# One core: the first RMS norm's factor moves from x to the outputs of two projections

## The reference

```python
def rms_norm(x, w, eps=NORM_EPS):
    xf = x.astype(jnp.float32)
    y = xf * lax.rsqrt(jnp.mean(xf * xf, axis=-1, keepdims=True) + eps)
    return (y * w.astype(jnp.float32)).astype(x.dtype)
...
        xn = rms_norm(h, norm_mix_pre[i])
        z = xn @ w_in[i]
        z_rwkv, z_gla = z[..., :RWKV_IN_WIDTH], z[..., RWKV_IN_WIDTH:]
        z_rwkv = z_rwkv + rwkv_mu[i] * (centred_shift(z_rwkv) - z_rwkv)
```

## Time and profile before

| what | value |
|---|---|
| median of 3 runs | 2900.9 us (2898.66 to 2914.93) |
| the profiled execution | 2904.88 us |
| its span | 2903.0 us |
| PE busy | 2746.3 us, 95% |
| VectorE busy | 1656.2 us, 57% |
| ScalarE busy | 1220.4 us, 42% |
| first matmul | 20.75 us |
| second block of `gla_project` begins on PE | 50.45 us |
| `rwkv_project`'s first matmul | 329.41 us |

### The profile page before, as it was taken

How to read it: one execution, slowest core, us unless ns; L and a number is a source line. 1 busy time by engine, 2 the same in 40 slices (tenths; PEclk the granted TensorE clock), 3 DMA queues, 4 the chain that set the end, 5 groups by cost and what they waited for, 6 DMA issues and landing times.

```text
span 2903.0 us, 57455 instructions
## 1 busy us (share of the span) xinstructions
PE 2746.3 (95%) x24688; PEld 2253.6 (78%) x24688; DVE 1656.2 (57%) x2482; ACT 1220.4 (42%) x2232; POOL 351.5 (12%) x472
## 2 busy tenths in 40 slices
PE   4997899898998999999999999999999999999997
PEld 3776677788886788788888888788887878888886
DVE  5669667345554566756543437675446765654343
ACT  4676666222322455433333335432235544333331
POOL 2000023444541001101000000000000100100000
PEclk9997899899998999999999999999999999999999
DMA  3420244211110334433344332222223443334432
GB/s 135 144 79 3 91 140 167 76 39 38 40 28 24 126 129 174 141 131 124 116 149 161 108 109 95 87 88 101 95 95 117 178 149 119 125 115 149 166 131 87
DMA packets 137821, 317.17 MB, mean 109 GB/s; under 512 B 13216, under 2 KB 40480, under 8 KB 137568
## 3 DMA queue, kind: packets, MB, share of 16 engines
q1 hardware_dynamic: 115344, 236.94, 24.1%
q0 software_dynamic: 22224, 76.56, 7.4%
HBM read 267.18 MB, written 46.14 MB: 108 GB/s over the span
## 4 chain that ended last, share of the span: by engine, by line
PE 62%; DVE 3%; DMA 1%; issue 1%; ACT 1%; POOL 0%; DVEq 0%; SPq 0%; ACTq 0%; POOLq 0%
PE be_ps L3297 20%; PE be_ps L3328 16%; PE be_ps L3223 16%; PE be_ps L3276 7%; PE be_ps L3350 1%; PE be_ps L2792 1%; DMA f_inner<-be_gate 0%; PE be_ps L2786 0%; ACT be_whi L3385 0%; DVE ext L2850 0%; DVE big L2829 0%; PE be_ps L2411 0%; DVE be_raw_r L3634 0%; DVE big L2819 0%; DMA be_raw<-in_w_out 0%
## 5 line engine op out<-in xcount | busy, mean ns | idle before, releaser
L3634 DVE TENSOR_TENSOR be_raw_r<-be_raw,be_whi 128x1024 fp32r<-128x1024 f32 x229 | 280.4, 1224 | 477.2 <-ACT be_whi L3385 476.9
L3385 ACT CAST be_whi<-be_raw 128x1024 fp32r<-128x1024 f32 x229 | 240.4, 1050 | 566.2 <-DMA be_raw<-in_ffn_down 298.2
L3328 PE MATMUL be_ps<-ext_r,be_whi 128*128 128x512 f32 x1152 | 356.4, 391 | 0.0
L3223 PE MATMUL be_ps<-ext_r,be_whi 128*128 128x512 f32 x896 | 278.9, 392 | 5.8 <-DVE be_raw_r L3634 3.1
L3297 PE MATMUL be_ps<-ext_r 128*128 128x512 f32 x832 | 278.3, 392 | 1.4 <-DVE be_ring L3708 1.4
L3328 PEld LDWEIGHTS be_ps<-ext_r,be_whi 128*128 128x128 f32 x1152 | 216.7, 188 | 44.8
L3297 PE MATMUL be_ps<-mid_r,ext_r 128*128 128x512 f32 x704 | 225.7, 396 | 1.3 <-DVE be_ring L3708 1.3
L3328 PE MATMUL be_ps<-ext_r,be_raw_r 128*128 128x512 f32 x576 | 224.7, 390 | 0.0
L3223 PEld LDWEIGHTS be_ps<-ext_r,be_whi 128*128 128x128 f32 x896 | 166.8, 188 | 45.4 <-DVE be_raw_r L3634 4.2
L3223 PE MATMUL be_ps<-big_r,be_whi 128*128 128x512 f32 x640 | 198.8, 392 | 0.0
L3297 PEld LDWEIGHTS be_ps<-ext_r 128*128 128x128 f32 x832 | 156.1, 188 | 38.6 <-DVE be_ring L3708 1.8
(11 more groups left out here) (412 smaller groups left out, 5531.2 us busy)
## 6 DMA issues: line engine op xcount, KB each, us to landing
be_raw<-in_ffn_down SPq DMA_DIRECT2D x88, 512.0 KB, 3.4
be_raw<-in_conv_in SPq DMA_DIRECT2D x48, 512.0 KB, 3.2
ext<-f_inner SPq DMA_DIRECT2D x72, 256.0 KB, 3.7
ext<-in_ffn_gate SPq DMA_DIRECT2D x30, 512.0 KB, 4.9
ext<-in_ffn_up SPq DMA_DIRECT2D x30, 512.0 KB, 4.1
gp_ada<-in_ada POOLq DMA_DIRECT2D x24, 512.0 KB, 3.6
rp_ada<-in_ada POOLq DMA_DIRECT2D x24, 512.0 KB, 3.9
be_raw<-in_ffn_gate SPq DMA_DIRECT2D x44, 256.0 KB, 2.7
```

What stands on the lines that cost most here:

```text
L3223: mm = pe.matmul(ps[:, bank], part[:, k * P:(k + 1) * P], xs(k), start=(k == order[0] and i == 0), stop=(k == order[-1] and i == 2))
L3328: mm = pe.matmul(ps[:, steps.bank[n, g]], part[:, at], x, start=(i % NPAIR == 0 and u == 0 and p == 0), stop=(i % NPAIR == NPAIR - 1 and u ...
L3385: act.copy(w.hi[:, n % 3], w.raw[:, n % 3]).then_inc(w.hi_ready, 1)
L3634: dve.tensor_tensor(w.lo(n), w.raw[:, n % 3], w.hi[:, n % 3].bitcast(F32), ALU.subtract).then_inc(w.lo_ready, 1)
```

## The change

x is loaded in eight pieces of two channel tiles, behind the vectors and the first weights and ahead of the constants. `xn_hi` and `xn_lo` are made from x times gain alone, so that PE's first tile does not wait for the norm. The squares, sums and roots are made beside PE's first two tiles, and the factor of each token is copied to `scale`, 128 by 1024. Each tile that leaves the banks is multiplied by `scale` on VectorE: in `gla_project` that takes the place of ScalarE's emptying (a gate's Silu then works in place), and in `rwkv_project` too, where `edge` now has one buffer, and ScalarE's multiplication by half of mu comes behind GpSimd's addition. `pre_norm` and `load_constants` as blocks are gone. The distribution of `ada` tiles over the steps of `gla_project` is another. The diff, cut to its core:

```diff
-def pre_norm(core, w, source, h, gain, xn_hi, xn_lo, c, acc):
...
+class FirstNorm:
...
+    def load(self, sp, hf, q):
+        pair = slice(2 * q, 2 * q + 2)
+        sp.dma_start(self.h[:, pair, self.cols(hf)], self.source[:, pair, self.cols(hf)]).then_inc(self.loaded[hf][q], 16)
+
+    def hi(self, act, hf, m):
+        act.wait_ge(self.loaded[hf][m // 2], 16)
+        act.activation(self.xn_hi[:, m, self.cols(hf)], self.h[:, m, self.cols(hf)], ACT.Copy, scale=self.gain[:, m:m + 1]
+                       ).then_inc(self.hi_done, 1)
+
+    def lo(self, dve, hf, m):
+
+        dve.wait_ge(self.hi_done, KD * hf + m + 1)
+        dve.scalar_tensor_tensor(self.xn_lo[:, m, self.cols(hf)], self.h[:, m, self.cols(hf)], self.gain[:, m:m + 1],
+                                 self.xn_hi[:, m, self.cols(hf)].bitcast(F32), ALU.mult, ALU.subtract
+                                 ).then_inc(self.lo_done, 1)
+
+    def square(self, act, hf, m):
+        act.activation(self.squares[hf][m], self.h[:, m, self.cols(hf)], ACT.Square).then_inc(self.squared, 1)
...
+    def take(self, act, hf):
+        act.wait_ge(self.spread, hf + 1)
+        act.copy(self.scale[:, self.cols(hf)], self.side[:, hf]).then_inc(self.scaled, 1)
...
@@ gla_project @@
-        modulation = Modulation(core, ctx, "gp", dram_ada, c, mod, 0, (3, 3, 2, 2, 2, 2, 2, 3, 0, 0, 3, 2), 9)
+        modulation = Modulation(core, ctx, "gp", dram_ada, c, mod, 0, (0, 1, 2, 2, 2, 3, 3, 3, 1, 1, 3, 3), 9)
...
+            sp.dma_start(core.vec[:, :], dram_vec).then_inc(norm.vec_loaded, 16)
+            load_weights(0)
+            for hf in two:
+                for q in range(KD // 2):
+                    norm.load(sp, hf, q)
+            load_weights(1)
+            sp.dma_start(core.const[:, :], dram_const[:, 0:N_STAY * P]).then_inc(norm.const_loaded, 16)
...
-            def drain(s):
-                act.wait_ge(filled, s + 1)
...
+            def finish_gate(s):
+                act.wait_ge(drained, s + 1)
+                act.activation(z[:, place(s)], z[:, place(s)], ACT.Silu)
...
+            weights_hi(0)
+            for hf in two:
+                for m in range(KD):
+                    norm.hi(act, hf, m)
+            weights_hi(1)
+            for m in range(KD):
+                norm.square(act, 0, m)
+            weights_hi(2)
+            for m in range(4):
+                norm.square(act, 1, m)
+            act.wait_ge(norm.const_loaded, 16)
+            norm.take_root(act, 0)
+            for m in (4, 5):
+                norm.square(act, 1, m)
+            norm.take(act, 0)
+            for m in (6, 7):
+                norm.square(act, 1, m)
+            norm.take_root(act, 1)
+            norm.take(act, 1)
+            for n in modulation.of_step(1):
+                modulation.scale(act, n)
...
+            def drain(s, hf=None):
+
+                part = slice(0, T) if hf is None else norm.cols(hf)
+                out = edge[:, s % 2, 1:T + 1] if is_conv(s) else z[:, place(s)]
+                dve.wait_ge(filled, s + 1)
+                dve.wait_ge(norm.scaled, 2 if hf is None else hf + 1)
+                ins = dve.tensor_tensor(out[:, part], acc[:, s % 2, part], scale[:, part], ALU.mult)
+                if hf != 0:
+                    ins.then_inc(drained, 1)
...
+            for s in range(2, n_tiles + 1):
                 if s + 1 < n_tiles:
                     weights_lo(s + 1)
...
+                drain(s - 1)
...
+            pool.wait_ge(norm.hi_done, 2 * KD)
             modulation.load(pool, 0, modulation.count)
...
@@ rwkv_project @@
-        edge = sb("edge", [P, 2, T + 2])
+        edge = sb("edge", [P, T + 2])
...
-            def drain(s):
-                act.wait_ge(filled, s + 1)
-                if s >= 2:
-                    act.wait_ge(summed, s - 1)
-                act.activation(edge[:, s % 2, 1:T + 1], acc[:, s % 2], ACT.Identity, scale=share[:, 1, ORDER[s]:ORDER[s] + 1]
-                               ).then_inc(edged, 1)
+            def share_around(s):
+                out = z[:, PLACE[ORDER[s]]]
+                act.wait_ge(summed, s + 1)
+                act.activation(out, out, ACT.Identity, scale=share[:, 1, ORDER[s]:ORDER[s] + 1]).then_inc(shared, 1)
...
+                if s == 7:
+                    decay_rates(2, 1)
                 if s:
-                    drain(s - 1)
+                    share_around(s - 1)
...
+            def drain(s):
+
+                dve.wait_ge(filled, s + 1)
+                if s:
+                    dve.wait_ge(summed, s)
+                    dve.wait_ge(mixed, s)
+                dve.tensor_tensor(edge[:, 1:T + 1], acc[:, s % 2], scale[:, :], ALU.mult).then_inc(edged, 1)
+
             def mix(s):
                 out = z[:, PLACE[ORDER[s]]]
-                dve.wait_ge(summed, s + 1)
-                dve.scalar_tensor_tensor(out, acc[:, s % 2], share[:, 0, ORDER[s]:ORDER[s] + 1], out, ALU.mult, ALU.add
+                dve.wait_ge(shared, s + 1)
+                dve.scalar_tensor_tensor(out, edge[:, 1:T + 1], share[:, 0, ORDER[s]:ORDER[s] + 1], out, ALU.mult, ALU.add
                                          ).then_inc(mixed, 1)
...
                 if s + 1 < NZR:
                     weights_lo(s + 1)
+                if s:
+                    drain(s - 1)
...
                 if s >= 2:
-                    pe.wait_ge(mixed, s - 1)
+                    pe.wait_ge(edged, s - 1)
```

More of the change, by code:

```diff
@@ L275, in parts @@
                                 for x in ("whi", "wlo"))
-        def flat(x):
-            return x[:, 0].rearrange("p k c -> p (k c)")
-        self.ahead = Ahead([(self.weights[self.first], flat(self.raw), flat(self.w_hi), flat(self.w_lo), self.loaded[0],
-                             self.hi_ready, self.lo_ready)])
     def w_hi_of(self, m):
@@ L731, in accumulate @@
                 dve.tensor_tensor_scan(x, mask, x, 0.0, ALU.mult, ALU.add).then_inc(summed, 1)
-            for s in range(n_tiles + 1):
+            dve.memset(edge[:, :, :], 0.0).then_inc(edged, 1)
+            dve.wait_ge(norm.vec_loaded, 16)
+            weights_lo(0)
+            for hf in two:
+                for m in range(KD):
+                    norm.lo(dve, hf, m)
+            weights_lo(1)
+            for m in range(1, KD):
+                norm.add(dve, 0, m)
+            for m in (1, 2, 3):
+                norm.add(dve, 1, m)
+            norm.invert(dve, 0)
+            for m in (4, 5):
+                norm.add(dve, 1, m)
+            drain(0, 0)
+            for m in (6, 7):
+                norm.add(dve, 1, m)
+            weights_lo(2)
+            norm.invert(dve, 1)
+            drain(0, 1)
+            for n in modulation.of_step(1):
+                modulation.add(dve, n)
+            dve.wait_ge(edged, 1)
+            for s in range(2, n_tiles + 1):
                 if s + 1 < n_tiles:
                     weights_lo(s + 1)
-                if s == 0:
-                    dve.memset(edge[:, :, :], 0.0).then_inc(edged, 1)
-                if s == 2:
-                    dve.wait_ge(edged, 1)
+                drain(s - 1)
                 if s == 10:
@@ L774, in decay_sum @@
                               ).then_inc(unit_made, 1)
-            for s in range(n_tiles):
+            pe.wait_ge(w.lo_ready, 1)
+            for hf in two:
+                for k in range(KD):
+                    pe.wait_ge(norm.lo_done, hf * KD + k + 1)
+                    for part_w, x in ((w.w_hi, xn_hi), (w.w_hi, xn_lo), (w.w_lo, xn_hi)):
+                        ins = pe.matmul(half(acc[:, 0], hf), part_w[:, 0, k], half(x[:, k], hf),
+                                        start=(k == 0 and part_w is w.w_hi and x is xn_hi),
+                                        stop=(k == KD - 1 and part_w is w.w_lo))
+            ins.then_inc(filled, 1)
+            for s in range(1, n_tiles):
                 pe.wait_ge(w.lo_ready, s + 1)
@@ L1187, in rwkv_project @@
         first_hi, fed_early, exp_table = sem("first_hi"), sem("fed_early"), sem("exp_table")
[L1188 removed]
+        filled, edged, summed, shared, mixed = (sem(x) for x in ("filled", "edged", "summed", "shared", "mixed"))
         ready, lora_loaded, keep_loaded, spread_loaded = (sem(x) for x in ("ready", "lora_loaded", "keep_loaded", "spread_loaded"))
```

234 lines of the change are left out of this document (68 added, 166 removed).

## The result

| what | before | changed |
|---|---|---|
| median of the runs made side by side (4 each) | 2905.6 us (2898.7 to 2914.9) | 2945.1 us (2943.2 to 2947.6) |
| the profiled execution, its span | 2904.9, 2903.0 us | 2944.3, 2942.5 us |
| PE busy | 2746.3 us, 95% | 2767.3 us, 94% |

The changed kernel takes 1.0131 times as long, with a 95% interval of 1.0110 to 1.0153. The forecast was 2931 us within 2908 to 2950, slower with a chance of 0.81. Sign and range held; the point lay 14 us low.

The account below looks back on a forecast made before the run. PE, busy 95% of the span, was taken as the bound. 2904.9-10.1 (front and gla_project)+37.5 (rwkv_project)+2.5 (clock) = 2934.8 us for the profiled execution, less 4.0 to the median: 2931 us, range 2908 to 2950.

Parts of the forecast that it names:

- The front: From the loads of x to tile 2 of gla_project: tile 2 begins at 39.0 us, 32.0 us earlier.
- gla_project: From tile 2 on, VectorE's longer rounds make PE wait; of the front's 32.0 us, 10.1 are left.
- the three places named: PE's waits in gla_project ahead of tiles 8, 9 and 12: 4.5, 6.7 and 4.1 us.
- rwkv_project: Longer chain through emptying, GpSimd and ScalarE's sharing: PE waits of 36.2 us and 1.3 for the tail, 37.5 lost.
- the carried figures: PE's waits in rwkv_project, from carrying orders, waits and row durations through the 15 steps; their sum is 36.2 us.
- the forecast's own sign: What would show it right: in rwkv_project PE idles some 36 us and the section takes 244 us instead of 207.
- the tail: End of rwkv_project: emptying, addition, sharing and mix add 1.3 us.
- The clock: Half-clock matmuls on PE after long waits in rwkv_project: 2.5 us added once, bounds 0 and 3 x 2.5.
- GpSimd's addition: In rwkv_project, taken at 1.95 us; 0.55 more in each of nine deciding rounds would be +5.
- Cancelling: Rival: in rwkv_project only the first two waits (10.6) and the tail remain, 2903 us; chance 0.09.
- faster: Rival: the front's gain reaches gla_project's end but for 4 us, rwkv_project loses 10; 2883 us, chance 0.06.
- The worse one: Rival: every long wait costs the clock and GpSimd is slower beside VectorE; +10, 2941 us, inside the range, no separate chance.

Follow-up runs that it names:

- e2: Changed kernel with gla_project's ada tiles spread flatter, two in each of steps 1 to 9 and three in 10 and 11; ratio 1.0118 to the kernel before.
- e9: Changed kernel with filler matmuls keeping PE busy through the waits in gla_project and rwkv_project; run once, 2931.4 us beside 2912.6 for the kernel before.

## Why the prediction was right in sign and low in size

- **The front.** PE began at 8.49 (9.5 forecast), tile 1 at 21.92 (22.9), and tile 2 at 39.24 us (39.0). Right.
- **gla_project.** Rounds with three `ada` tiles took 18.4 us (forecast 18.3), that with one 10.9 (10.6). PE waited 4.46, 3.71 and 1.94 us at the three places named, where 4.5, 6.7 and 4.1 were forecast; the missing part went into slower matmuls in between. The end gained 10.6 us (10.1). Right, and e2 shows the cause that was named. That `gla_mix` would be 1.7 us shorter was not foreseen.
- **rwkv_project.** Six of the seven waits came at the places named: 4.83, 4.81, 2.88, 5.83, 5.73, 0.74 for 4.3, 6.3, 3.3, 8.1, 9.6, 1.0; the one at tile 5 (3.6) was 0.22. (For the first the forecast's own rows give 360.57+4.5-360.95 = 4.1.) Their sum is 25.0, not 36.2, because PE's slower stretches fill part of the same gaps. With PE kept at full clock nearly everywhere (e9) the carried figures come back: tiles 2, 4, 5, 7, 8, 9 and 11 are 4.8, 7.9, 2.2, 3.3, 8.5, 9.6 and 1.8 us longer than before, where 4.3, 6.3, 3.6, 3.3, 8.1, 9.6 and 1.0 were forecast. From tile 1 on e9 is 39.6 us longer, where 37.5 was forecast: the tail took 0.8 instead of 1.3, and the tiles 38.8 instead of 36.2, of which 2.6 stay open. By the forecast's own sign, from the first matmul to the end of the last `mix`, 244 us instead of 207 was said, and 254.6 instead of 206.1 measured.
- **The clock: the term that was mis-sized.** I wrote "I add 2.5 once; the bounds are 0 and 3 x 2.5", for "a PE that is slower then arrives later at the next wait, which shrinks". e9 measured 8.2 us. The argument fits `gla_project` and fails in `rwkv_project`, where waits stand in the middle of tiles. The price of one stretch was low as well: the earlier trace rows has 0.69 over 9.55 busy us, which is 3.0 us and not 2.5, and the section's tile 0 took 2.9 us more at 0.69 than at 1.00. My upper bound of 7.5 comes near the 8.2 by luck: it counted three waits over 6 us, and there were none, but five of 2.88 to 5.83 that each cost clock. The Trainium skill, "TensorE: Matmul & The Clock Gate", Part 1, says that the slow state is the default and that activity releases it. This case's trace agrees, as in the 2.07 us of small products behind the wait at 465.24.
- **GpSimd's addition** took 1.89 us in the section, so the up to 5 us for a slower one were rightly left out of the point.
- **The rest of the kernel**, taken as unchanged, was 3.8 us longer in the two executions, in stages that scatter by more. Together: 2.2 better ahead of the section, 8.0 worse in it, 3.8 worse behind: 9.6, for the 9.5 us by which the execution exceeds my 2934.8. The 4 us that I took off for the median were no property of the kernel: with a fourth run its median was 2905.6. That the total fell inside the range owes something to the 2.2 us that went the other way.
- **The rivals.** Cancelling and faster fell with the waits. The worse one, "every long wait costs the clock and GpSimd is slower", 2941, came nearest, by its first half.
